# First stage by halves, and plan loads moved, in a hybrid layer with experts on one NeuronCore

## The reference

```python
mod = jax.nn.silu(c) @ W_ada[l] + b_ada[l]
sh1, sc1, gt1, sh2, sc2, gt2 = jnp.split(mod[:, None, :], 6, axis=-1)
h = rmsnorm(x, norm1_g[l]) * (1 + sc1) + sh1
mix, sr, shg = token_mixer(h, ...)          # h @ W_in, retention and HGRN2 heads, @ W_out
x = x + (gt1 * mix).astype(x.dtype)
h = rmsnorm(x, norm2_g[l]) * (1 + sc2) + sh2
ff = hier_moe(h, ...)                       # top-1 group, then top-2 of its 4 experts
x = x + (gt2 * ff).astype(x.dtype)
...
y = y + combine[:, e:e + 1] * ((jax.nn.silu(xt @ W_gate_e[e]) * (xt @ W_up_e[e])) @ W_down_e[e])
```

## Time and profile before

| | |
|---|---|
| median of 3 runs | 1334.56 us (1333.1 to 1338.49) |
| the profiled execution's own time | 1333.58 us |
| its span | 1331.8 us |
| PE busy | 1081.6 us, 81% |
| DVE busy | 721.0 us, 54% |
| ACT busy | 602.1 us, 45% |
| POOL busy | 118.9 us, 9% |
| transfers | 210.62 MB, mean 158 GB/s |

### The profile page before, as it was taken

The page is one execution under the profiler, slowest core; times in us unless marked ns, Lnnn a source line. Parts: engine busy times, 40 slices in busy tenths (PEclk is TensorE's granted clock), DMA queues, the critical chain, the costliest instruction groups (busy, mean ns, idle before and its releaser), DMA issues. The chain is left out here.

```text
span 1331.8 us, 26478 instructions
## 1 busy us (share of the span) xinstructions
PE 1081.6 (81%) x8764; PEld 894.4 (67%) x8765; DVE 721.0 (54%) x1327; ACT 602.1 (45%) x1214; POOL 118.9 (9%) x241
## 2 busy tenths in 40 slices
PE   4188999889989999989948999349999998999900
PEld 4188788877879777877836877236777666767700
DVE  2712555135641456235645665756886675767449
ACT  4433444334543444334443221156776564656334
POOL 0200000000000000000000011210001001111042
PEclk8689999889999999999978999669999999999955
DMA  8421421122220421223217241288998896989175
GB/s 339 154 70 37 120 76 55 35 68 77 77 57 28 132 80 33 61 68 105 76 39 225 96 143 60 67 307 258 376 393 296 284 321 225 343 277 344 76 243 202
DMA packets 202260, 210.62 MB, mean 158 GB/s; under 512 B 15596, under 2 KB 169060, under 8 KB 201892
## 3 DMA queue, kind: packets, MB, share of 16 engines
q1 hardware_dynamic: 180640, 176.16, 40.2%
q0 software_dynamic: 5712, 18.23, 4.0%
q10 hardware_dynamic: 15828, 15.05, 3.2%
HBM read 185.32 MB, written 24.08 MB: 157 GB/s over the span
## 5 line engine op out<-in xcount | busy, mean ns | idle before, releaser
L735 PE MATMUL mixers_ps_proj<-early_h_hi,mixers_w_hi 128*128 128x352 f32 x256 | 86.3, 337 | 39.9 <-ACT mixers_steps L548 27.7
L2015 PE MATMUL experts_ps_g<-experts_w_hi,experts_x_hi 128*128 128x512 f32 x256 | 106.4, 416 | 14.5 <-DVE experts_w_lo L1848 10.4
L1848 DVE TENSOR_TENSOR experts_w_lo<-experts_raw_more,experts_w_hi 128x2048 fp32r<-128x2048 f32 x48 | 108.3, 2285 | 9.1 <-ACT experts_w_hi L1728 9.1
L1848 DVE TENSOR_TENSOR experts_w_lo<-all_raw,experts_w_hi 128x2048 fp32r<-128x2048 f32 x48 | 109.5, 2283 | 6.5 <-ACT experts_w_hi L1728 6.5
L1728 ACT ACTIVATE experts_w_hi<-all_raw 128x2048 fp32r<-128x2048 f32 x48 | 91.6, 1912 | 38.3 <-PE experts_ps_g L2017 34.3
L763 PE MATMUL mixers_ps_proj<-mixers_w_hi,early_h_hi 128*128 128x512 f32 x256 | 107.2, 419 | 0.0
L948 DVE TENSOR_TENSOR mixers_w_lo<-all_raw,mixers_w_hi 128x1024 fp32r<-128x1024 f32 x32 | 38.7, 1223 | 121.9 <-ACT mixers_w_hi L543 121.9
L765 PE MATMUL mixers_ps_proj<-mixers_w_hi,early_h_lo 128*128 128x512 f32 x256 | 101.4, 396 | 0.0
L2017 PE MATMUL experts_ps_g<-experts_w_hi,experts_x_lo 128*128 128x512 f32 x256 | 101.3, 396 | 0.0
L764 PE MATMUL mixers_ps_proj<-mixers_w_lo,early_h_hi 128*128 128x512 f32 x256 | 101.1, 395 | 0.0
L2016 PE MATMUL experts_ps_g<-experts_w_lo,experts_x_hi 128*128 128x512 f32 x256 | 101.1, 395 | 0.0
(11 more groups left out here) (319 smaller groups left out, 2678.8 us busy)
## 6 DMA issues: line engine op xcount, KB each, us to landing
experts_raw_more<-in_W_down_e_dram SPq DMA_DIRECT2D x128, 256.0 KB
all_raw<-in_W_gate_e_dram SPq DMA_DIRECT2D x96, 256.0 KB, 6.1
all_raw<-in_W_up_e_dram SPq DMA_DIRECT2D x96, 256.0 KB, 6.8
all_raw<-in_W_in_dram SPq DMA_DIRECT2D x32, 512.0 KB, 4.0
all_raw<-in_W_ada_dram SPq DMA_DIRECT2D x32, 512.0 KB, 5.3
condition_w_ada_in<-in_W_ada_dram SPq DMA_DIRECT2D x4, 2048.0 KB, 10.5
experts_raw_more<-in_W_gate_e_dram SPq DMA_DIRECT2D x32, 256.0 KB
experts_raw_more<-in_W_up_e_dram SPq DMA_DIRECT2D x32, 256.0 KB
```

The costliest lines, as they stand in the source:

```text
L735: pe.matmul(out, whi, xhi, start=(k == 0), stop=False)
L1848: dve.tensor_tensor(w_lo[:, 2 * p:2 * p + 2], raw_pair[p], f32(w_hi[:, 2 * p:2 * p + 2]), ALU.subtract).then_inc(lo_done, 1)
L2015: pe.matmul(out, x_hi[:, k, :], w_hi[:, c, at], start=(k == 0), stop=False)
```

## The change

*Experts.* In the loop over the experts, ACT and PE loaded four values of the plan at the head of each expert: count and place of the rests of this expert and of the next. Now they load this expert's count and its end (`x + 65`, so that no sum is needed) behind ACT's first split and at PE's k == 4, and the next expert's count later; its place is the end of this one. Three loads instead of four. Ahead of the loop one load instead of two. POOL and DVE have as many as before.

*First stage.* Four buffers for x instead of three; SP sends x0 to x3 first, then two lumps, x4 to x7, unit 0, the third lump, the sample's tile, the fourth lump, then the other units and tables. The lumps come in the order 0, 2, 1, 3, so that the first two hold shift and scale of the blocks k = 0 to 3. `h` is made in two halves of four blocks: DVE shifts blocks 0 and 2 (4 and 6) and ACT blocks 1 and 3 (5 and 7); ACT makes all high parts, DVE all low parts, POOL none. The sample's part is made for four blocks at once. Unit 0 of `W_in` is split in this stage into tiles of its own (`w0_hi`, `w0_lo`), and PE multiplies it here, k outermost (`first_unit`), behind each half; the three PSUM tiles of its pieces are shared with the mixers.

*Mixers.* The multiplication of unit 0 ahead of the loop is gone, and so is its split. The semaphores that it would have raised are primed higher; SP raises the four for raw units itself, ahead of the table's transfer, and POOL's list begins with those that are waited for first.

```diff
 def phase_condition(nc, s):
+        XB = 4
...
-        xt = sb("xt", [P, 3, D])
+        xt = sb("xt", [P, XB, D])
...
+            for i in range(XB):
+                x_tile(i)
+            for n in range(2):
+                lump(n)
+            for i in range(XB, NP_T):
+                x_tile(i)
+            unit(0, unit_in)
+            lump(2)
+            x_tile(NP_T)
+            lump(3)
+            for u in range(1, 4):
+                unit(u, fetched)
...
+            def shifted(k, step):
+                act.activation(h32[:, k, 0:SEQ], h32[:, k, 0:SEQ], ACT.Identity, scale=gain[:, k, 0:1],
+                               bias=mod_col[:, k, 0:1]).then_inc(hi_done, 1)
+                act.wait_ge(hi_done, step)
+            def high_parts(g):
+                k, done = 4 * g, 7 * g
+                act.wait_ge(gain_done, 2 * g + 2)
+                shifted(k + 1, done + 1)
+                act.wait_ge(h_done, 4 * g + 2)
+                act.activation(s.h_hi[:, k:k + 4, SEQ:NTOK], s.h_sample[:, k:k + 4, :], ACT.Copy).then_inc(hi_done, 1)
+                act.wait_ge(h_done, 4 * g + 3)
+                high(k)
+                high(k + 1)
+                shifted(k + 3, done + 5)
+                act.wait_ge(h_done, 4 * g + 4)
+                high(k + 2)
+                high(k + 3)
...
+            act.activation(s.w0_hi[:, :, :], s.raw[:, 0].rearrange("p (k n) -> p k n", k=KD), ACT.Copy)\
+               .then_inc(unit_hi, 1)
+            high_parts(0)
+            high_parts(1)
...
+            def first_unit(g):
+                if g == 0:
+                    pe.wait_ge(unit_lo, 1)
+                    pe.wait_ge(xlow, NT)
+                    pe.wait_ge(xhigh, NT)
+                for k in range(4 * g, 4 * g + 4):
+                    pe.wait_ge(lo_done, 5 * g + (k - 4 * g) + 2)
+                    for c in range(3):
+                        some, out = slice(c * PIECE, (c + 1) * PIECE), bank[c][:, 0:PIECE]
+                        pe.matmul(out, s.w0_hi[:, k, :], s.h_hi[:, k, some], start=(k == 0), stop=False)
+                        pe.matmul(out, s.w0_hi[:, k, :], s.h_lo[:, k, some], start=False, stop=False)
+                        pe.matmul(out, s.w0_lo[:, k, :], s.h_hi[:, k, some], start=False, stop=(k == KD - 1))
...
+            for i in range(XB):
+                turn_x(i)
+            for n in range(2):
+                lump(n)
+            for i in range(XB, NT):
+                turn_x(i)
+                if i == XB:
+                    turn_mod(0)
+            lump(2)
+            first_unit(0)
+            lump(3)
+            turn_mod(1)
+            first_unit(1)
...
+            sample(0)
+            shifted(0)
+            dve.wait_ge(unit_hi, 1)
+            dve.tensor_tensor(s.w0_lo[:, :, :], s.raw[:, 0].rearrange("p (k n) -> p k n", k=KD), f32(s.w0_hi[:, :, :]),
+                              ALU.subtract).then_inc(unit_lo, 1)
+            shifted(2)
+            low_parts(0)
+            copy_mod(2)
+            copy_mod(3)
+            gains(1)
+            sample(1)
+            shifted(4)
+            shifted(6)
+            low_parts(1)
-        @block.gpsimd
-        def _(pool):
-            for k in range(1, KD, 2):
-                pool.wait_ge(hi_done, k + 1)
-                pool.tensor_tensor(s.h_lo[:, k, :], h32[:, k, :], f32(s.h_hi[:, k, :]), ALU.subtract)
...
 def phase_mixers(nc, s):
+            for u in (1, 2, 3, 0):
+                sp.sem_inc(raw_in[u], 16 + PRIMED)
             sp.dma_start(decay.rearrange("p c l -> p (c l)"), a["consts"][:, N_KEPT + N_TABLES:])\
               .then_inc(fetched, 16)
-            for u in range(4):
-                sp.sem_inc(raw_in[u], 16)
...
+            for semaphore in (hi_done, lo_done):
+                pool.sem_inc(semaphore, PRIMED + 1)
+            pool.sem_inc(t_done, PRIMED + 3)
             for semaphore in primed:
                 pool.sem_inc(semaphore, PRIMED)
...
-            for u in range(2):
-                split(u, PRIMED, None)
+            split(1, PRIMED, None)
...
             pe.wait_ge(cleared, 2)
-            for c in range(3):
-                turned_piece(0, c, PRIMED + 1, None)
...
 def phase_experts(nc, s):
-            return plan(e, val(e, x + 32), COLS - 1), plan(e, val(e, x + 64), 2 * NTOK // REST)
+            return plan(e, val(e, x + 32), COLS - 1), plan(e, val(e, x + 65), 2 * NTOK // REST)
...
         @block.scalar
...
             def tile(x):
-                m, before = rests(act, x)
-                end = act.snap(before + m)
-                if not last:
-                    m_next, before_next = rests(act, after)
...
                 pair(0)
+                m, end = rests(act, x)
                 with act.If(m > 0):
                     rest_turned(end)
                 silu(0)
                 pair(1)
+                m_next = None if last else plan(act, act.snap(x + 33), COLS - 1)
                 with act.If(m > 0):
                     rest_out(x, end, m)
...
         @block.tensor
...
             def tile(x):
-                m, before = rests(pe, x)
-                end = pe.snap(before + m)
-                if not last_expert:
-                    after = pe.snap(x + 1)
-                    m_next, before_next = rests(pe, after)
...
                     if half == 1:
+                        m_next = None if last_expert else plan(pe, pe.snap(x + 33), COLS - 1)
                         with pe.If(m > 0):
                             rest_down(x, end)
...
                         if k == 4:
                             if half == 1:
                                 turn_h(0)
                             else:
+                                m, end = rests(pe, x)
                                 with pe.If(m > 0):
                                     rest_turn(end)
```

More of the change, by code:

```diff
@@ new lines, in lump @@
+            def lump(n):
+                pe.wait_ge(w_in[n % 2], 16 * (n // 2 + 1))
+                if n >= 2:
+                    pe.wait_ge(ada_copied, n - 1)
+                for k in range(KD):
+                    for q in range(4):
+                        last = pe.matmul(ps_ada[n % 2][32 * q:32 * q + 32, 0:P], s.cT[:, k, :],
+                                         w_ada[:, n % 2, k, q * P:(q + 1) * P], start=(k == 0), stop=(k == KD - 1))
+                last.then_inc(ada_done, 1)
@@ new lines, in sample @@
+            def sample(g):
+                k = 4 * g
+                dve.wait_ge(gain_done, 2 * g + 2)
+                dve.wait_ge(xlow, NT)
+                dve.wait_ge(xhigh, NT)
+                part = s.h_sample[:, k:k + 4, :]
+                dve.tensor_tensor(part, h32[:, k:k + 4, SEQ:NTOK], gain[:, k:k + 4, 1:2].broadcast_to([P, 4, DEC]),
+                                  ALU.mult).then_inc(h_done, 1)
+                dve.wait_ge(h_done, 4 * g + 1)
+                dve.tensor_tensor(part, part, mod_col[:, k:k + 4, 1:2].broadcast_to([P, 4, DEC]), ALU.add)\
+                   .then_inc(h_done, 1)
@@ L395, in phase_mixers @@
         ada_row = sb("ada_row", [P, 2, P])
-        ps_p = [ps(f"ps_proj{n}", [P, 512]) for n in range(2)]
+        ps_p, ps_d = s.ps_p, s.ps_d
         ps_tr = ps("ps_tr", [P, 4, P])
@@ L1688, in gather_rests @@
             def gather_rests(x, first):
-                m, before = rests(pool, x)
+                m = plan(pool, val(pool, x + 32), COLS - 1)
+                before = plan(pool, val(pool, x + 64), 2 * NTOK // REST)
                 with pool.If(m > 0):
@@ L1813, in tile @@
                 if not last:
-                    rest_front(after, m_next, before_next)
+                    rest_front(after, m_next, end)
                 h_high(1)
@@ L1835, in _ @@
             x_high(0)
-            m, before = rests(act, 0)
+            m = plan(act, 32, COLS - 1)
+            none = act.snap(m * 0)
             with act.If(m > 0):
-                rest_in(act.snap(before + 1))
-            rest_front(0, m, before)
+                rest_in(act.snap(none + 1))
+            rest_front(0, m, none)
             for p in range(3, PAIRS):
@@ L1858, in rest_product @@
             def rest_product(x):
-                m, before = rests(dve, x)
+                m = plan(dve, val(dve, x + 32), COLS - 1)
+                before = plan(dve, val(dve, x + 64), 2 * NTOK // REST)
                 with dve.If(m > 0):
```

236 lines of the change are left out of this document (121 added, 115 removed).

## The result

The changed kernel takes 1300.22 us (median of 4 runs, 1296.62 to 1302.95), the kernel before in the same comparison 1333.83 us (1332.87 to 1338.49). The ratio is 0.9742, interval [0.9718, 0.9767]. Forecast were 1301 us and a range of 1295 to 1313.

The account below looks back on a forecast made before the run. PE, busy 81% of the span, was taken as the bound, with gaps in both changed places. Gains of 21.0 + 12.7 = 33.7 us off 1333.58 gave 1299.9; the median's 1.0 more made 1300.9, forecast 1301, range 1295 to 1313.

Parts of the forecast that it names:

- Heads of the experts: PE's waits at expert heads: moving its four plan loads removes the gap whole, 14 x 0.74 = 10.4 us.
- The waits at L1955: PE's 8 waits ahead of L1955, 10.3 us: they go once ACT's loads move; gain 9.2, bounds 5 and 9.7.
- the sum: Expert loop: 10.4 + 9.2 + 1.9 - 0.5 = 21.0 us gained.
- Head of the first expert: PE's 4.1 us wait before L2015 falls to about 2.1; gain 1.9 us, bounds 1 and 2.5.
- Cover at k == 4: PE's two loads at k == 4, first half of an expert: 4.7 us of cover against 1.6, cost 0.
- Weights: Expert loop: weight transfers, already 395 GB/s in experts without rests, become late next; 0.5 us taken off the gain.
- First stage: Start to unit 1 of the mixers: new order and h by halves gain 12.7 us, bounds 4.3 and 15.3.
- Rival 1: First stage: half rate in all of the first unit, ending at 72; gain 4.3, time 1309 us; chance 0.11.
- ACT's shift: First stage, making h: ACT's shift with scale and bias from SBUF taken as 1.05 us, bounds 1.03 and 1.15.
- The rule that spoke against it: First stage: short bursts with waits can find PE's clock lowered each time; the first unit would then end at 72.
- Start of the mixers and the counts: Unit 1 starts 7.4 us after the phase begins; POOL's 55 counts cost nothing; the gain is carried from there.

## Why the prediction was right, point by point

**Heads of the experts: right mechanism, term too small.** 10.4 was forecast, from the row's 14 x 0.74. Undoing this step alone costs 13.9 in the experts, 12.3 at equal clock. The windows over the whole loop show where the rest hides. In the kernel before:

```profile
886.20:1263.20 377.00, 351.93 (x2281) 267.71 (x2281) 253.55 (x196) 232.74 (x237) 36.89 (x46) 0.99 0.86 295
```

In the changed kernel:

```profile
875.80:1229.20 353.40, 346.95 (x2281) 267.68 (x2281) 254.52 (x196) 234.38 (x238) 39.92 (x47) 0.99 0.90 317
```

Idle time fell from 25.1 to 6.45, by 18.6; 19.1 had been forecast. But PE's busy time, for the same 2281 records, fell too, by 5.0. Of these 0.8 is the clock (5.9 against 4.3 us at 1.2 GHz, half counts). That is 0.16 + 0.10 for each, 14 x 0.26 = 3.6. The kernel with PE's loads back has them again: at equal clock (half of the time at 1.2 GHz taken off) PE's busy time is 348.3 to 349.0 us in the three executions with PE's loads at the head and 344.2 to 345.2 in the ten without them and without further loads. So a wait of 0.74 in the row costs 1.0, and undoing the step, expert by expert, gave the same (1.04 to 1.16). It does not hold for every wait: the kernel with ACT's loads back has eight waits ahead of the rest's down product, 17.1 us, its busy time is 345.1, and at equal clock its experts are 17.1 longer than the changed kernel's; there the row is about the price.

**The waits at L1955: right.** 9.2 of 10.3 were to go; the row is 1.2 now. Not foreseen was that these waits would have grown to 17.1 if only PE's loads had been moved: the sum treated the two edits as independent and was right only because both were made.

**Head of the first expert: right.** 1.9 forecast, 1.88 measured, 2.2 left where 2.1 was expected.

**Cover at k == 4: right.** Cost 0; the cover forecast as 4.7 us is 4.0, and the two experiments with further loads bracket it between 3.1 and 6.2.

**Weights: right in kind, too small.** 0.5 was taken off for the stretch of experts without rests. The fourth and the fifth expert gained next to nothing (0.38 and 0.14 us). They have as many matmuls as the third, which takes 17.72, and take 18.42 and 18.65: some 1.6 us lost. ACT now waits for raw weights in the loop, and the transfers stand at 394 GB/s in the window from 932 to 950 us (395 before). ACT's waits in the changed kernel:

```profile
ACT experts_w_hi L1834 <- DMA all_raw<-in_W_up_e_dram: 3.1, 4, 1.7
```

In the fourth expert it reaches PE so: ACT's split begins late, `h_hi` stands behind it on ACT, DVE's `h_lo` behind that, and the down product waits (0.40 here, 0.63 in the fifth: the row of `ps_y` above):

```profile
951.73 1.92 ACT L1834 ACTIVATE experts_w_hi<-experts_raw_more 128x2048 fp32r<-128x2048 f32 x1 [0.54 <-DMA experts_raw_more<-in_W_up_e_dram]
...
954.50 0.49 PE L2139 MATMUL experts_ps_y<-experts_w_hi,experts_h_hi 128*128 128x512 f32 x1 [0.40 <-DVE experts_h_lo L1987]
```

**First stage: 12.7 forecast, 9.7 measured; two terms were mis-sized.** The first is the transfers: "at 416 GB/s" was taken from a window in which nothing else moves. Over the whole stretch from 7 to 36 us it is 387 GB/s; the 11.14 MB up to the sample's tile then take 28.8 us instead of 26.8, and the tile lands at 36.04. All that hangs on it moves by 2.2. (The prediction's terms from landing to `h` add up to 37.6, not to the 37.8 that it goes on with; measured are 4.0 us for them. Rival 1's second half, by its own terms, ends at 71.4 and not 72.) The second is the clock: the forecast took 1.2 GHz for the first k of each half. In the first half PE was at full rate almost from the start (0.85 us better), in the second at 1.2 GHz for 6 us (1.9 us worse). With 7.56 instead of 7.7 to unit 1 that makes 3.2 of later start, and it is the difference. The clock's part is that of this execution: in the eight with this first stage unit 0 ends at 66.4 to 68.0, and in three of them 3.2 to 3.8 us of the first half are at 1.2 GHz.

The steps in between came out as worked: from the start of the first half to PE's first product 4.83 (4.8 forecast), from the end of the first half to the second half's first product 7.25 (7.2), `steps` 3.7 us behind its transfer (3.6), 12 matmuls of unit 1 at half rate (13). DVE's shift lasts 0.81 in all its instances; the 2.90 of the earlier trace rows is gone with POOL's work beside it.

**ACT's shift: outside both bounds.** 1.03 to 1.15 were given, from rows without scale and bias in SBUF. Group of the four, and of the plain copies of the same size:

```profile
L242 ACT ACTIVATE early_h_hi<-condition_h 128x1024 fp32r<-128x1024 f32 x8 | 8.0, 1046 | 0.1
L237 ACT ACTIVATE condition_h<-condition_h,condition_mod_col,condition_gain 128x1024 f32<-128x1024 f32 x4 | 4.9, 1231 | 6.7 <-DVE condition_gain L401 6.7
```

It takes 1.23, 0.19 more than a copy. The Trainium skill, ScalarE: Activation LUTs, section "What ACT_TABLE_LOAD costs", gives 186 ns and 0.833 ns an element, and some 93 ns more for each operand that is a column in SBUF: an estimate of 1.04 and 1.23, and both rows agree. The forecast's bounds were too narrow because the nearest rows had one such operand at most. It costs DVE 0.8 us of idle time ahead of the third low part of each half, where 0.5 had been forecast.

**The rule that spoke against it: half right.** PE's pauses in the first stage are 1.72 us ahead of the first half, with full clock from 45 us on, and 4.29 ahead of the second, with 1.2 GHz for 6 us; with a pause of 1.44 in the experiments with the fourth lump first the second half was at full clock. Over the eight executions with this first stage the second half has 3.3 to 6.2 us at 1.2 GHz in each; the first half, behind pauses of 1.7 to 2.1, has none in five and 3.2 to 3.8 in three. By the rule of the Trainium skill, TensorE: Matmul & The Clock Gate, section "HAM oscillation — how this bites in real kernels", bursts with waits between them can find the clock lowered at every burst. Here that holds for the burst behind the long pause; behind the short one it came out either way, and in this trace the clock did not fall inside a half. The end of unit 0, 66.94, lies between the forecast (63.6) and rival 1 (72).

**Start of the mixers and the counts: right.** The gain is carried: with half of the time at 1.2 GHz taken off, the rest of the mixers takes 579.0 us before and 576.9 to 581.9 in the kernels with the new first stage. The order of the counts is worth nothing, as costed.

## What to carry to other kernels

A wait of a matmul stream can cost more than its row: compare starts with starts, or look whether "busy" time falls when the wait goes. Two waits in a row, one behind the other, are one price: what the first gives back the second may take, so cost them together, and undo them one at a time to see it. Values that the sequencer must load were free here as long as it ran ahead of its array: read in the trace when the loads run and when the first instruction that needs them starts, and place them where that distance is longest.

## What the runs showed of the hardware

- Waits in the middle of otherwise dense matmuls brought TensorE's clock to 1.2 GHz with PE busy on both sides: in the kernel with six more loads behind seven of the sixteen at k == 4, and behind one for `rest_x` (27.5 us more at half rate in its experts, 13.8 us lost). Their length alone does not tell which: the seven have 1.9 to 3.0 us, the nine others 1.1 to 3.1. The waits of 0.7 to 1.9 us of the kernel before left it at 2.4 GHz (5.9 us at half rate in 377, all in the first expert).
- The rest of the mixers, the same instructions each time, takes 592.4 to 601.0 us in the 14 profiled executions, and the time at 1.2 GHz in it is 24.9 to 42.4 us. Less half of that it is 576.9 to 581.9. Gains of 3 us, like that of the sample's tile sent earlier, drown in this. The four versions with the first stage in another order have 38.1 to 42.4 us at 1.2 GHz there, the eight executions with the order of the changed kernel 24.9 to 33.0, which gives back some 5 us of what the order gains; whether the order does this, or chance, no run settles (the kernel before has 38.4, the same mixers with the expert part alone 29.4).
- From 3.1 us of sequencer time at k == 4 (no cost) to 6.2 the price rises to 3.0 us for each expert, more than the 2.1 by which the loads exceed their cover, since the clock goes down as well.
